# Three regroupings in a two-block transformer kernel: forget-gate panels first, memory-key sums between panels, and the inverse's transpose taken by turning

## The chip, the cores and the metric

The kernel runs on one core of one Trainium2 chip. The metric is the device time of one execution in microseconds, as the median of several runs. Five engines work side by side on the core, each through its own queue in order: TensorE (PE; its weight loads are PEld), VectorE (DVE), ScalarE (ACT), GpSimd (POOL) and SyncE (SP, which here only issues loads). They meet only at semaphores.

## The reference, cut to what matters

256 tokens of width 1024 run through two blocks in float32. The first block has four feed-forward layers, a mixer with a gated delta rule and retention, and a mixer with dilated and differential attention. The second has two layers, each with block-sparse attention, a gated recurrence (HGRN) and attention to 256 memory rows. The change touches three things.

The recurrence of the second block (`lb` is 0 in layer 0):

```
lb_all = jnp.cumsum(jax.nn.softmax(hgrn_lb_logits, axis=0), axis=0); lb_all = lb_all - lb_all[0:1]
qf = jax.nn.silu(q)
log_f = jnp.logaddexp(jnp.log(lb), jnp.log1p(-lb) + jax.nn.log_sigmoid(fl))
kf = (1.0 - lb) * jax.nn.sigmoid(-fl)
```

The keys of the memory: `km = rms_norm(k_m.reshape(B, M, MEM_HEADS, MEM_HEAD_DIM), mem_k_norm[l])`.

The delta rule, which for each tile of 128 tokens and each of four heads needs the inverse of a 128 by 128 unit triangular matrix. The kernel builds it from the 16 by 16 blocks on the diagonal, and then doubles the size of the block three times (steps s = 0, 1, 2).

## The kernel before, in words

All weights are cut on the host into panels of 128 by 2048 (1 MB). A panel passes four engines. SP loads it into one of three raw buffers. ACT rounds it to a high part (`split_hi`, L1557; in two halves `half_hi`, L1566). DVE forms the low part as the difference (`split_lo`, L1872; halves `half_lo`, L1855). PE multiplies it with the activations, which are split in the same way, in three products: L1047, L1048, L1049 for projections, 48 matmuls for a panel, 24 for a half. ACT then evacuates the result from PSUM (`evacuate`, L1657). A panel's split is queued three panels before its product.

The order of everything is written out once, in `order()`, as one list of steps (engine, kind, arguments); each engine walks through its own steps in that list, and waits for the step of another engine by its place in the list (`at`). `panel_list` gives the steps of a row of panels; `rounds` and `merge` lay chains of small steps side by side in rounds; `halves` cuts panels into two half products; `weave` puts these between the rounds, so that PE has a product while the small steps wait for each other.

**Second block, start of a layer.** Panels 0 and 1 of `in2_l` give the recurrence's q (with Silu on ACT), panels 2 and 3 its forget gate `fh`, 4 and 5 its values. After panel 3 ACT loads the table set of Exp and Ln (`logs`), and `last_mixer` begins:

- `f_abs` (DVE, L2217 and L2218): minus the absolute value of `fh`; in layer 1 also four operations on the logits of `lb`.
- `f_ln` (ACT, L1796 and L1797): Exp, then Ln of one plus that; in layer 1 the same on eight columns (L1799, L1800).
- `f_log` (DVE, L2231; L2239 is its last line): the logarithm of the sigmoid; in layer 1 also `lb` applied and the input of the second logarithm, seven operations; last the input of `k_gate`.
- layer 1 only: `f_ln2` (ACT, L1805 and L1806) and `f_log2` (DVE, L2244 and L2245).
- `k_gate` (ACT, L1810), `cum_f` (DVE, four scans L2250), `diagonal` (PE, L1304: two tiles of four heads, 16 matmuls), `diagonal_in` (DVE, L2256).
- then eight levels of `gap_f` (L2269, L2270), `decay_f` (ACT), `q_level` (DVE, L2279), `k_level` (POOL), `level` (PE, L1304), `level_in` (L2287), one for every two half panels.

The norm of the memory keys (units `sk0`, `sk1` of a layer) goes through the same first rounds: `cn_sq` (ACT square, L1747), `cn_sum` (PE with a matrix of ones, L1451), `cn_rstd` (ACT, L1755 and L1756), `cn_use` (DVE, L2125). In layer 1 PE's queue is: panels 0 to 3, half (4,0), `cn_sum` 0, half (4,1), `cn_sum` 1, halves (5,0), (5,1), (6,0), (6,1), `diagonal`, (7,0) ...

**First block, doubling of the inverse.** `m_mat` is the inverse so far, `t_mat` its transpose, both kept up to date. For each step and tile: `double_y` (PE: corner times `m_mat`), `y` (ACT copy from PSUM, L1710), `double` (PE: `t_mat` times y, and for s < 2 a second product that gives the transpose's correction), `doubled` (DVE, L2063: the subtraction on `m_mat`, and for s < 2 on `t_mat`). All products of four heads go through `heads` (L1304). A product of four heads is eight matmuls in the trace, a transpose of four heads is four. At the end of the stretch stand `evacuate` of `in0`'s panel 13 on ACT and `ret_out` on PE, which waits for it.

Of the kernel before, what the change touches and what calls it, by code (L numbers as in the profile page):

```python
# [345 lines left out]
def delta_rounds():  # L346
# [10 lines left out]
    for s in range(3):  # L357
        doubling += [both(("pe", "double_y", s), ("act", "y", s)),
                     both(("pe", "double", s), ("dve", "doubled", s), *([("pool", "corner", s + 1)] if s < 2 else []))]
# [8 lines left out]
def delta_tail():  # L368

    o = BASE["out0"]  # L370
    pe = [("double_y", 2, 0), ("double_y", 2, 1), ("double", 2, 0), ("double", 2, 1), ("ret_out", 0), ("ret_out", 1), ("u", 0),
          ("cn_sum", ("ro", 0)), ("state",), ("ret_out", 2), ("from_state",), ("ret_out", 3), ("u", 1), ("cn_sum", ("ro", 1)),
          ("delta_out", 0), ("delta_out", 1), ("out_part", "out0", 0, 0, 2), ("cn_sum", ("do", 0)), ("out_part", "out0", 0, 2, 4),
          ("cn_sum", ("do", 1)), ("out_part", "out0", 0, 4, 8), ("panel", "out0", 1), ("panel", "out0", 2), ("panel", "out0", 3)]
    act = [("y", 2, 0), ("y", 2, 1), ("evacuate", "in0", 13), ("half_hi", o + 1, 0), ("half_hi", o + 1, 1), ("cn_sq", ("ro", 0)), ("v_new", 0),
           ("cn_rstd", ("ro", 0)), ("state_copy",), ("half_hi", o + 2, 0), ("cn_sq", ("ro", 1)), ("v_new", 1), ("cn_rstd", ("ro", 1)),
           ("half_hi", o + 2, 1), ("cn_sq", ("do", 0)), ("cn_sq", ("do", 1)), ("cn_rstd", ("do", 0)), ("cn_rstd", ("do", 1)),
           ("split_hi", o + 3), ("split_hi", o + 4), ("split_hi", o + 5)]
    dve = [("doubled", 2, 0), ("doubled", 2, 1), ("half_lo", o + 1, 0), ("half_lo", o + 1, 1), ("v_less",), ("cn_use", ("ro", 0)),
           ("cn_use", ("ro", 1)), ("half_lo", o + 2, 0), ("half_lo", o + 2, 1), ("cn_use", ("do", 0)), ("cn_use", ("do", 1)),  # L380
           ("split_lo", o + 3), ("split_lo", o + 4)]
    return [(e, k, tuple(a)) for e, steps in (("pe", pe), ("act", act), ("dve", dve)) for k, *a in steps]


def hgrn_rounds(l):

    out = [[("dve", "f_abs", (l,)), ("act", "f_ln", (l,))], [("dve", "f_log", (l,))]]
    if l:
        out += [[], [("act", "f_ln2", (l,)), ("dve", "f_log2", (l,))]]
    out += [[("act", "k_gate", (l,)), ("dve", "cum_f", (l,))], [("pe", "diagonal", (l,)), ("dve", "diagonal_in", (l,))]]  # L390
# [31 lines left out]
def last_mixer(l):  # L422
# [6 lines left out]
    chains = [rounds(NORM_COLS, [(f"sk{l}", 0), (f"sk{l}", 1)]), hgrn,  # L429
# [54 lines left out]
def order():  # L484
# [49 lines left out]
    for l in range(2):  # L534
# [7 lines left out]
        angles = {1: [("dve", "angle", ())], 3: [("act", "sines", ())]} if l == 0 else None  # L542
        out += panel_steps(f"in2_{l}", angles, 0, 4) + [("act", "logs", ())] + last_mixer(l)
# [29 lines left out]
def build(nc, x_in, mem_in, pos_in, panels, gains, small_in, tab0, tab1, tab2, tab3, out):  # L573
    with ExitStack() as ctx:
# [248 lines left out]
        for k in range(2):  # L823
# [6 lines left out]
            for l in range(2):  # L830
                dest[f"in2_{l}", k] = (blocks(qh, k), "cols", ACT.Silu)
                dest[f"in2_{l}", 2 + k] = (blocks(fh, k), "cols", ACT.Copy)
# [132 lines left out]
        def _(sp):  # L965
# [9 lines left out]
            def load_panel(n):  # L975
# [10 lines left out]
                else:  # L986
                    source = {"gate": b + 3 * i - 1 if i else b, "up": b + 3 * i if i else b + 1, "both": b + 3 * UPS - 1, None: n}[kind]
                    if b == BASE["out0"]:
                        source = b + (n - b + 2) % 4
# [54 lines left out]
        def _(pe):  # L1044
# [330 lines left out]

            def double(s, t):
                pe.wait_ge(act_done, at("act", "y", s, t))
                ins = heads(ps[:, delta_bank(t, 1)], lambda h: t_mat[:, t, h], lambda h: pw_a[:, t, h])
                if s < 2:
                    ins = heads(ps[:, delta_bank(t, 0)], lambda h: pw_a[:, t, h], lambda h: t_mat[:, t, h])  # L1380
                ins.then_inc(pe_done, 1)
# [140 lines left out]
            def hgrn_out(l, g):  # L1522
                pe.wait_ge(dve_done, at("dve", "level_in", l, 7))
                for i in range(2):
# [10 lines left out]
                         "turn_m": turn_m, "kq": kq, "double_y": double_y, "double": double, "u": u, "state": state_mm,  # L1535
# [6 lines left out]
        def _(act):  # L1542
# [188 lines left out]

            def v_new_(t):
                act.wait_ge(pe_done, at("pe", "u", t))
                copy_back(v_new[:, t], t)
# [58 lines left out]
            def f_ln(l):  # L1793
# [4 lines left out]
                if l:  # L1798
# [13 lines left out]
            def decay_f(l, v):  # L1812
# [6 lines left out]
                          "decay": decay, "pow2_n": pow2_n, "pow4_n": pow4_n, "pow8_a": pow8_a, "t_rows": t_rows, "y": y,  # L1819
# [6 lines left out]
        def _(dve):  # L1826
# [259 lines left out]
            def doubled(s, t):  # L2086

                dve.wait_ge(pe_done, at("pe", "double", s, t))
                if s < 2:
                    add_to(t_mat[:, t], delta_bank(t, 0), ALU.subtract)  # L2090
# [123 lines left out]
            def f_abs(l):  # L2214

                dve.wait_ge(act_done, at("act", "evacuate", f"in2_{l}", 3))
                step(ts(hg[1], fh, -1.0, None, ALU.mult))  # L2217
                step(tt(hg[1], fh, hg[1], ALU.min))  # L2218
                if l:
# [8 lines left out]
            def f_log(l):  # L2228
# [3 lines left out]
                if l:  # L2232

                    step(stt(lbl, lbd, 0.0, lbn, ALU.min, ALU.subtract))
                    step(tt(hg[1], hg[1], along(lbl[:, 4:8], SEQ), ALU.add))
                    step(tt(hg[2], hg[1], along(lbl[:, 0:4], SEQ), ALU.subtract))
                    step(ts(hg[3], hg[2], -1.0, None, ALU.mult))
                    step(tt(hg[2], hg[2], hg[3], ALU.min))
# [42 lines left out]
            def level_in(l, v):  # L2281
# [6 lines left out]
                else:  # L2288
# [12 lines left out]
                          "angle": angle, "f_abs": f_abs, "f_log": f_log, "f_log2": f_log2, "cum_f": cum_f,  # L2301
# [73 lines left out]
```

## Time and profile before

| what | before |
|---|---|
| median of 3 runs (lowest, highest) | 1566.8 us (1565.97, 1567.17) |
| the profiled execution's own time | 1568.67 us |
| its span in the trace | 1566.7 us |
| PE, DVE, ACT, POOL busy, share of the span | 96%, 75%, 49%, 6% |
| granted clock of PE, mean | 0.997 of 2.4 GHz |

The span is the time from the first to the last instruction of one execution. A row of a timeline gives the start, the duration, the engine, the line of the kernel, and in square brackets how long the engine stood idle before it and which engine's result ended that. Matmuls overlap: the queue moves on before one has ended. Consecutive instructions of one line are merged, with their count behind x.

### The profile page before, as it was taken

How to read it: one execution, taken by the hardware profiler on the slowest of the kernel's cores; microseconds unless marked ns; L12 is line 12 of the kernel's file. 1: busy time of each engine (PE TensorE's matmuls, PEld its weight loads, DVE VectorE, ACT ScalarE, POOL GpSimd, SP SyncE). 2: the span in 40 equal slices, each digit the busy share in tenths (PEclk: the TensorE clock that was granted, in tenths of full speed). 3: DMA queues.
4: the chain of work that ended last, by engine and by line, in shares of the span. 5: the costliest groups of instructions: out<-in, count | busy, mean ns of one | idle time of the engine just before them, and what ended most of it. 6: DMA issues, size and time to landing. Idle time of an engine off the chain costs nothing.

```text
span 1566.7 us, 23942 instructions
## 1 busy us (share of the span) xinstructions
PE 1504.3 (96%) x9974; PEld 1347.7 (86%) x9974; DVE 1177.0 (75%) x1393; ACT 762.6 (49%) x931; POOL 94.1 (6%) x66
## 2 busy tenths in 40 slices
PE   7999999999999999999998999999999989989988
PEld 6888899988888888888886888889999869879967
DVE  6878668757887788787676788777779676579674
ACT  5433456435433453334545533345664675555662
POOL 2000000011000000000000100002013001003000
PEclk9999999999999999999999999999999999999999
DMA  7655534214655545555441465554444325434202
GB/s 263 213 188 188 180 132 174 81 55 157 212 189 200 177 173 188 191 189 185 170 153 55 162 212 189 189 188 162 155 169 137 106 82 187 162 110 161 108 28 81
DMA packets 51888, 246.76 MB, mean 157 GB/s; under 512 B 4619, under 2 KB 5771, under 8 KB 27718
## 3 DMA queue, kind: packets, MB, share of 16 engines
q1 hardware_dynamic: 50662, 238.29, 43.8%
q0 software_dynamic: 1120, 6.96, 1.2%
q8 instruction: 79, 1.29, 0.3%
q14 instruction: 27, 0.22, 0.0%
HBM read 244.18 MB, written 1.05 MB: 157 GB/s over the span
## 4 chain that ended last, share of the span: by engine, by line
PE 75%; DVE 13%; ACT 7%; issue 2%; DVEq 0%; ACTq 0%; POOL 0%
PE ps L1096 19%; PE ps L1098 9%; PE ps L1047 9%; PE ps L1049 9%; PE ps L1048 9%; PE ps L1149 8%; PE ps L1304 4%; PE ps L1150 4%; DVE w_lo L1872 3%; ACT w_hi L1557 2%; DVE act_two L1980 1%; ACT work L1766 1%; PE ps L1451 1%; ACT act_two L1635 1%; PE ps L1440 1%
## 5 line engine op out<-in xcount | busy, mean ns | idle before, releaser
L1557 ACT ACTIVATE w_hi<-raw 128x2048 fp32r<-128x2048 f32 x186 | 355.2, 1913 | 394.4 <-PE ps L1098 274.5
L1872 DVE TENSOR_TENSOR w_lo<-raw,w_hi 128x2048 fp32r<-128x2048 f32 x186 | 432.7, 2331 | 138.6 <-ACT w_hi L1557 135.9
L1096 PE MATMUL ps<-act_two,w_hi 128*128 128x512 f32 x1408 | 444.4, 397 | 5.0 <-DVE w_lo L1872 2.4
L1047 PE MATMUL ps<-act_two,w_hi 128*128 128x256 f32 x1120 | 327.8, 293 | 9.9 <-DVE act_two L1980 5.3
L1098 PEld LDWEIGHTS ps<-act_two,w_lo 128*128 128x128 f32 x1408 | 265.2, 188 | 63.0
L1048 PE MATMUL ps<-act_two,w_hi 128*128 128x256 f32 x1120 | 316.7, 283 | 0.0
L1049 PE MATMUL ps<-act_two,w_lo 128*128 128x256 f32 x1120 | 316.7, 283 | 0.0
L1098 PE MATMUL ps<-act_two,w_lo 128*128 128x256 f32 x1408 | 277.2, 278 | 0.0
L1047 PEld LDWEIGHTS ps<-act_two,w_hi 128*128 128x128 f32 x1120 | 214.6, 192 | 16.2 <-issue 5.4
L1096 PEld LDWEIGHTS ps<-act_two,w_hi 128*128 128x128 f32 x1408 | 215.1, 189 | 7.9 <-DVE w_lo L1872 3.6
L1048 PEld LDWEIGHTS ps<-act_two,w_hi 128*128 128x128 f32 x1120 | 214.7, 192 | 3.7 <-issue 3.6
L1049 PEld LDWEIGHTS ps<-act_two,w_lo 128*128 128x128 f32 x1120 | 214.5, 192 | 0.0
L1149 PE MATMUL ps<-g_two,w_hi 128*128 128x512 f32 x384 | 136.2, 398 | 0.0
L1855 DVE TENSOR_TENSOR w_lo<-raw,w_hi 128x1024 fp32r<-128x1024 f32 x76 | 103.9, 1393 | 26.2 <-ACT w_hi L1566 24.9
L1149 PE MATMUL ps<-act_two,w_hi 128*128 128x512 f32 x320 | 113.3, 398 | 3.1 <-DVE act_two L1911 2.5
L1150 PE MATMUL ps<-g_two,w_lo 128*128 128x256 f32 x384 | 107.5, 280 | 0.0
L1047 PE MATMUL ps<-w_hi,act_two 128*128 128x256 f32 (+1 forms) x336 | 106.1, 316 | 0.2 <-ACT work L1654 0.2
L1048 PE MATMUL ps<-w_lo,act_two 128*128 128x256 f32 (+1 forms) x336 | 100.1, 298 | 0.0
L1049 PE MATMUL ps<-w_hi,act_two 128*128 128x256 f32 (+1 forms) x336 | 100.1, 298 | 0.0
L1031 POOL TENSOR_TENSOR pair<-pair 128x512 f32<-128x512 f32 x27 | 41.0, 1520 | 860.3 <-ACT pair L1614 859.5
L1150 PE MATMUL ps<-act_two,w_lo 128*128 128x256 f32 x320 | 89.5, 280 | 0.0
L1149 PEld LDWEIGHTS ps<-g_two,w_hi 128*128 128x128 f32 x384 | 72.1, 188 | 16.9
(287 smaller groups left out, 2007.0 us busy)
## 6 DMA issues: line engine op xcount, KB each, us to landing
raw<-panels SPq DMA_DIRECT2D x184, 1024.0 KB, 4.8
raw<-panels SPq DMA_DIRECT2D x80, 512.0 KB, 4.8
raw<-panels SPq DMA_DIRECT2D x8, 256.0 KB, 6.3
table<-tab POOLq DMA_DIRECT2D x1, 1472.0 KB, 9.5
table<-tab POOLq DMA_DIRECT2D x1, 1216.0 KB, 5.5
xn<-x_in SPq DMA_DIRECT2D x4, 256.0 KB, 5.8
work<-mem_in POOLq DMA_DIRECT2D x1, 1024.0 KB, 9.0
xn<-mem_in POOLq DMA_DIRECT2D x1, 1024.0 KB, 5.2
```

Of the source, the lines that this page charges most:

```text
L1031: nc.gpsimd.tensor_tensor(pair[:, 0:512], pair[:, 0:512], pair[:, 512 * b:512 * b + 512], ALU.add).then_inc(pool_done, 1)
L1047: pe.matmul(o, l[0], r[0], start=start, stop=False, skip_group_check=shared)
L1048: pe.matmul(o, l[0], r[1], start=False, stop=False, skip_group_check=shared)
L1049: return pe.matmul(o, l[1], r[0], start=False, stop=stop, skip_group_check=shared)
L1096: pe.matmul(grid(ps[:, bank + half], 2), w[half][0], act_two[:, slots[c]], start=c == 0, stop=False)
L1098: ins = pe.matmul(ps[:, bank + half, 0:SEQ], w[half][1], act_hi[:, slots[c]], start=False, stop=c == DC - 1)
L1149: pe.matmul(grid(ps[:, bank], 2), hi, two, start=first and m == 0, stop=False)
L1150: ins = pe.matmul(ps[:, bank, 0:SEQ], lo, two[:, 0], start=False, stop=last and m == len(quarters) - 1)
L1304: ins = pe.transpose(oh, lhs(h), ident) if turn else pe.matmul(oh, lhs(h), rhs(h), start=True, stop=True)
L1557: nc.scalar.activation(w_hi[:, s], raw[:, s], ACT.Copy).then_inc(panel_hi, 1)
L1855: ins = tt(w_lo[:, s, c], raw[:, s, c], w_hi[:, s, c].bitcast(F32), ALU.subtract)
L1872: tt(w_lo[:, s], raw[:, s], w_hi[:, s].bitcast(F32), ALU.subtract).then_inc(panel_lo, 1)
```

## The change

- The weights of the forget gate become panels 0 and 1 of `in2_l`, those of q (Silu) panels 2 and 3. SP loads the first four panels in rotated order; the host's layout stays.
- `f_abs` runs on DVE beside panel 2, after that panel's queued `split_lo`, as one operation on `fh` instead of two.
- The small operations for `lb` (four on DVE in `f_abs`, two on ACT in `f_ln`, the last on DVE in `f_log`) are done in layer 0 and kept for layer 1.
- In layer 1 `f_log` has three operations: it leads straight to the second logarithm. Two others, `lb` added and the input of `k_gate`, become the step `f_gate`, which DVE does after it. `f_ln2` stands on ACT behind the evacuation of panel 4 and its splits, as before.
- The squares of the memory keys stand on ACT after the splits beside panels 0 and 1, their sums on PE behind panels 1 and 2. `cn_rstd` of the two units follows in `f_log`'s round (in layer 1 the second follows `f_ln2`), and both `cn_use` come after `cum_f` on DVE.
- In the delta rule `double` has one product in all steps. For s = 1 and 2, `turn_again` on PE turns `m_mat` into PSUM behind `double_y`, and `t_again` on ACT copies it to `t_mat` behind `y`; `double` waits for it.

The diff, without the lines that only register the new steps:

```diff
@@ -355,7 +355,7 @@
     for s in range(3):
-        doubling += [both(("pe", "double_y", s), ("act", "y", s)),
+        doubling += [both(("pe", "double_y", s), *([("pe", "turn_again", s)] if s else []), ("act", "y", s), *([("act", "t_again", s)] if s else [])),
                      both(("pe", "double", s), ("dve", "doubled", s), *([("pool", "corner", s + 1)] if s < 2 else []))]
@@ -368,11 +368,11 @@
     o = BASE["out0"]
-    pe = [("double_y", 2, 0), ("double_y", 2, 1), ("double", 2, 0), ("double", 2, 1), ("ret_out", 0), ("ret_out", 1), ("u", 0),
+    pe = [("double_y", 2, 0), ("turn_again", 2, 0), ("double_y", 2, 1), ("turn_again", 2, 1), ("double", 2, 0), ("double", 2, 1), ("ret_out", 0), ("ret_out", 1), ("u", 0),
           ("cn_sum", ("ro", 0)), ("state",), ("ret_out", 2), ("from_state",), ("ret_out", 3), ("u", 1), ("cn_sum", ("ro", 1)),
           ("delta_out", 0), ("delta_out", 1), ("out_part", "out0", 0, 0, 2), ("cn_sum", ("do", 0)), ("out_part", "out0", 0, 2, 4),
           ("cn_sum", ("do", 1)), ("out_part", "out0", 0, 4, 8), ("panel", "out0", 1), ("panel", "out0", 2), ("panel", "out0", 3)]
-    act = [("y", 2, 0), ("y", 2, 1), ("evacuate", "in0", 13), ("half_hi", o + 1, 0), ("half_hi", o + 1, 1), ("cn_sq", ("ro", 0)), ("v_new", 0),
+    act = [("y", 2, 0), ("t_again", 2, 0), ("y", 2, 1), ("t_again", 2, 1), ("evacuate", "in0", 13), ("half_hi", o + 1, 0), ("half_hi", o + 1, 1), ("cn_sq", ("ro", 0)), ("v_new", 0),
            ("cn_rstd", ("ro", 0)), ("state_copy",), ("half_hi", o + 2, 0), ("cn_sq", ("ro", 1)), ("v_new", 1), ("cn_rstd", ("ro", 1)),
@@ -384,10 +384,13 @@
 
-    out = [[("dve", "f_abs", (l,)), ("act", "f_ln", (l,))], [("dve", "f_log", (l,))]]
+    key_norm = [[("act", "cn_rstd", ((f"sk{l}", g),)), ("dve", "cn_use", ((f"sk{l}", g),))] for g in (0, 1)]
+    out = [[("act", "f_ln", (l,))], [("dve", "f_log", (l,)), key_norm[0][0]]]
     if l:
-        out += [[], [("act", "f_ln2", (l,)), ("dve", "f_log2", (l,))]]
-    out += [[("act", "k_gate", (l,)), ("dve", "cum_f", (l,))], [("pe", "diagonal", (l,)), ("dve", "diagonal_in", (l,))]]
+        out += [[("dve", "f_gate", (l,))], [("act", "f_ln2", (l,)), ("dve", "f_log2", (l,)), key_norm[1][0]]]
+    else:
+        out[1] += key_norm[1][:1]
+    out += [[("act", "k_gate", (l,)), ("dve", "cum_f", (l,)), key_norm[0][1], key_norm[1][1]], [("pe", "diagonal", (l,)), ("dve", "diagonal_in", (l,))]]
     ahead = len(out)
@@ -426,7 +429,7 @@
     h = n + 7
-    chains = [rounds(NORM_COLS, [(f"sk{l}", 0), (f"sk{l}", 1)]), hgrn,
+    chains = [hgrn,
               [[]] * n + rounds(NORM_COLS, qk + [(f"ho{l}", 0), (f"ho{l}", 1)]),
@@ -539,8 +542,12 @@
         out += [product] + scaled(f"pre{l}") + [evacuate] + late
-        angles = {1: [("dve", "angle", ())], 3: [("act", "sines", ())]} if l == 0 else None
-        out += panel_steps(f"in2_{l}", angles, 0, 4) + [("act", "logs", ())] + last_mixer(l)
+        square, total = [[(e, k, ((f"sk{l}", g),)) for g in (0, 1)] for e, k in (("act", "cn_sq"), ("pe", "cn_sum"))]
+        beside = {0: square[:1], 1: total[:1] + square[1:], 2: total[1:] + [("dve", "f_abs", (l,))], 3: []}
+        if l == 0:
+            beside[1] = beside[1] + [("dve", "angle", ())]
+            beside[3] = [("act", "sines", ())]
+        out += panel_steps(f"in2_{l}", beside, 0, 4) + [("act", "logs", ())] + last_mixer(l)
         if l == 0:
@@ -828,8 +835,8 @@
             for l in range(2):
-                dest[f"in2_{l}", k] = (blocks(qh, k), "cols", ACT.Silu)
-                dest[f"in2_{l}", 2 + k] = (blocks(fh, k), "cols", ACT.Copy)
+                dest[f"in2_{l}", k] = (blocks(fh, k), "cols", ACT.Copy)
+                dest[f"in2_{l}", 2 + k] = (blocks(qh, k), "cols", ACT.Silu)
                 dest[f"in2_{l}", 4 + k] = (rows(ih, k), "rows", ACT.Copy)
@@ -986,6 +993,8 @@
                     if b == BASE["out0"]:
+                        source = b + (n - b + 2) % 4
+                    if b in (BASE["in2_0"], BASE["in2_1"]) and n - b < 4:
                         source = b + (n - b + 2) % 4
@@ -1373,12 +1382,13 @@
 
+            def turn_again(s, t):
+                pe.wait_ge(dve_done, at("dve", "doubled", s - 1, t))
+                heads(ps[:, delta_bank(t, 1)], lambda h: m_mat[:, t, h], None, turn=True).then_inc(pe_done, 1)
+
             def double(s, t):
-                pe.wait_ge(act_done, at("act", "y", s, t))
-                ins = heads(ps[:, delta_bank(t, 1)], lambda h: t_mat[:, t, h], lambda h: pw_a[:, t, h])
-                if s < 2:
-                    ins = heads(ps[:, delta_bank(t, 0)], lambda h: pw_a[:, t, h], lambda h: t_mat[:, t, h])
-                ins.then_inc(pe_done, 1)
+                pe.wait_ge(act_done, at("act", "t_again" if s else "y", s, t))
+                heads(ps[:, delta_bank(t, 1)], lambda h: t_mat[:, t, h], lambda h: pw_a[:, t, h]).then_inc(pe_done, 1)
 
@@ -1729,6 +1739,10 @@
 
+            def t_again(s, t):
+                act.wait_ge(pe_done, at("pe", "turn_again", s, t))
+                copy_back(t_mat[:, t], delta_bank(t, 1))
+
             def v_new_(t):
@@ -1795,7 +1809,7 @@
                 ins = nc.scalar.activation(hg[1], hg[1], ACT.Ln, bias=cst("one"))
-                if l:
+                if not l:
                     step(nc.scalar.activation(lbn, lbn, ACT.Exp))
@@ -2086,8 +2100,6 @@
                 dve.wait_ge(pe_done, at("pe", "double", s, t))
-                if s < 2:
-                    add_to(t_mat[:, t], delta_bank(t, 0), ALU.subtract)
                 finish(add_to(m_mat[:, t], delta_bank(t, 1), ALU.subtract))
@@ -2213,10 +2225,9 @@
 
-                dve.wait_ge(act_done, at("act", "evacuate", f"in2_{l}", 3))
-                step(ts(hg[1], fh, -1.0, None, ALU.mult))
-                step(tt(hg[1], fh, hg[1], ALU.min))
-                if l:
+                dve.wait_ge(act_done, at("act", "evacuate", f"in2_{l}", 1))
+                step(stt(hg[1], fh, -1.0, fh, ALU.mult, ALU.min))
+                if not l:
                     a, b = sm("lb", 0, 4), sm("lb", 4, 4)
@@ -2230,12 +2241,16 @@
                 if l:
-
+                    step(tt(hg[2], hg[1], along(lbd[:, 0:4], SEQ), ALU.add))
+                    finish(stt(hg[2], hg[2], -1.0, hg[2], ALU.mult, ALU.min))
+                else:
+                    tt(k_g, hg[1], fh, ALU.subtract)
                     step(stt(lbl, lbd, 0.0, lbn, ALU.min, ALU.subtract))
-                    step(tt(hg[1], hg[1], along(lbl[:, 4:8], SEQ), ALU.add))
-                    step(tt(hg[2], hg[1], along(lbl[:, 0:4], SEQ), ALU.subtract))
-                    step(ts(hg[3], hg[2], -1.0, None, ALU.mult))
-                    step(tt(hg[2], hg[2], hg[3], ALU.min))
+                    finish(tt(lbd[:, 0:4], lbl[:, 4:8], lbl[:, 0:4], ALU.subtract))
+
+            def f_gate(l):
+
+                step(tt(hg[1], hg[1], along(lbl[:, 4:8], SEQ), ALU.add))
                 finish(tt(k_g, hg[1], fh, ALU.subtract))
```

## Rows read from the trace of the kernel before

**Rows 1.** The page: busy times, and the chain that ended last by engine.
```profile
PE 1504.3 (96%) x9974; PEld 1347.7 (86%) x9974; DVE 1177.0 (75%) x1393; ACT 762.6 (49%) x931; POOL 94.1 (6%) x66
...
PE 75%; DVE 13%; ACT 7%; issue 2%; DVEq 0%; ACTq 0%; POOL 0%
```

**Rows 2.** Windows: length, PE, PEld, DVE, ACT, POOL busy, clock, DMA.
```profile
1112.00:1150.00 38.00, 38.00 (x309) 37.04 (x309) 27.57 (x36) 26.42 (x29) 0.00 (x0) 1.00 0.44 152
...
1366.00:1398.00 32.00, 24.82 (x181) 23.26 (x180) 23.35 (x28) 20.34 (x25) 0.00 (x0) 0.95 0.29 99
...
1396.00:1397.00 1.00, 1.00 (x7) 1.00 (x6) 1.00 (x2) 1.00 (x2) 0.00 (x0) 0.50 0.00 0
```

**Rows 3.** Timeline of PE: delta rule, then both layers.
```profile
312.41 1.53 PE L1304 MATMUL ps<-const,work 128*128 128x128 f32 x12 [0.23 <-DVE work L2063]
...
337.38 1.95 PE L1304 MATMUL ps<-work 128*128 128x128 f32 x16
...
1149.39 1.95 PE L1304 MATMUL ps<-work 128*128 128x128 f32 x16
...
1372.35 1.12 PE L1451 MATMUL ps<-pair,const 128*128 128x512 f32 x2 [1.55 <-ACT pair L1747]
...
1378.61 1.13 PE L1451 MATMUL ps<-pair,const 128*128 128x512 f32 x2 [2.27 <-ACT pair L1747]
...
1394.60 3.65 PE L1304 MATMUL ps<-work 128*128 128x128 f32 x16 [3.35 <-ACT work L1810]
...
1398.00 0.37 PE L1047 MATMUL ps<-act_two,w_hi 128*128 128x256 f32 x1
...
1415.35 1.95 PE L1304 MATMUL ps<-work,xn 128*128 128x128 f32 x16
...
1422.90 1.95 PE L1304 MATMUL ps<-work,xn 128*128 128x128 f32 x16
```

**Rows 4.** Timeline of ACT: delta rule, then layer 1.
```profile
338.47 0.60 ACT L1710 ACTIVATE work<-ps 128x512 f32<-128x512 f32 x1 [8.85 <-PE ps L1304]
...
1356.44 0.60 ACT L1657 ACTIVATE work<-ps 128x512 f32<-128x512 f32 x1 [1.74 <-PE ps L1049]
...
1368.45 1.90 ACT L1557 ACTIVATE w_hi<-raw 128x2048 fp32r<-128x2048 f32 x1
...
1370.37 1.28 ACT L1685 ACT_TABLE_LOAD   x1
...
1371.67 0.63 ACT L1747 ACTIVATE pair<-work 128x512 f32<-128x512 f32 x1
...
1375.37 1.06 ACT L1796 ACTIVATE work<-work 128x1024 f32<-128x1024 f32 x1 [3.07 <-DVE stat L2226]
...
1376.46 1.15 ACT L1797 ACTIVATE work<-work,const 128x1024 f32<-128x1024 f32 x1
```

**Rows 5.** Timeline of DVE: layer 0, then layer 1.
```profile
1143.53 1.22 DVE L2239 TENSOR_TENSOR work<-work 128x1024 f32<-128x1024 f32 x1
...
1370.39 2.29 DVE L1872 TENSOR_TENSOR w_lo<-raw,w_hi 128x2048 fp32r<-128x2048 f32 x1 [3.47 <-ACT w_hi L1557]
...
1379.90 0.75 DVE L2125 SCALAR_TENSOR_TENSOR work<-work,small,pair 128x512 f32<-128x512 f32 x1 [4.56 <-ACT pair L1756]
...
1388.70 2.36 DVE L1855 TENSOR_TENSOR w_lo<-raw,w_hi 128x1024 fp32r<-128x1024 f32 x2
...
1394.63 2.43 DVE L2250 TENSOR_TENSOR_SCAN work<-table,work 128x256 f32<-128x256 f32 x4
...
1398.28 1.29 DVE L2256 TENSOR_TENSOR work<-ps,const 128x512 f32<-128x512 f32 x2
...
1410.28 1.23 DVE L2279 TENSOR_TENSOR work<-work,pair 128x1024 f32<-128x1024 f32 x1
...
1417.31 1.22 DVE L2279 TENSOR_TENSOR work<-work,pair 128x1024 f32<-128x1024 f32 x1
```

**Rows 6.** Chain of waits, delta rule: start, duration, what.
```profile
319.90 3.57 PE ps L1304 x32
```

More of the change, by code:

```diff
@@ L1534, in _ @@
                          "turn_k": turn_k, "kk": kk, "turn_a": turn_a, "pow2": pow2, "pow4": pow4, "pow8": pow8, "pow16": pow16,
-                         "turn_m": turn_m, "kq": kq, "double_y": double_y, "double": double, "u": u, "state": state_mm,
+                         "turn_m": turn_m, "kq": kq, "double_y": double_y, "double": double, "turn_again": turn_again, "u": u, "state": state_mm,
                          "from_state": from_state, "delta_out": delta_out, "ret_scores": ret_scores, "ret_out": ret_out,
@@ L1818, in _ @@
                           "evacuate": evacuate, "silu": silu, "logs": logs_and_exps, "tap": tap, "conv_silu": conv_silu, "ab_exp": ab_exp, "softplus": softplus,
-                          "decay": decay, "pow2_n": pow2_n, "pow4_n": pow4_n, "pow8_a": pow8_a, "t_rows": t_rows, "y": y,
+                          "decay": decay, "pow2_n": pow2_n, "pow4_n": pow4_n, "pow8_a": pow8_a, "t_rows": t_rows, "t_again": t_again, "y": y,
                           "v_new": v_new_, "state_copy": state_copy, "cn_sq": cn_sq, "cn_rstd": cn_rstd, "exp": exp_,
@@ L2300, in _ @@
                           "gate_out": gate_out, "y_lo": y_lo, "mask_max": mask_max, "divide": divide, "lam_mul": lam_mul, "lam": lam,
-                          "angle": angle, "f_abs": f_abs, "f_log": f_log, "f_log2": f_log2, "cum_f": cum_f,
+                          "angle": angle, "f_abs": f_abs, "f_log": f_log, "f_log2": f_log2, "f_gate": f_gate, "cum_f": cum_f,
                           "diagonal_in": diagonal_in, "gap_f": gap_f, "q_level": q_level, "level_in": level_in})
```

## The prediction, made before the changed kernel ran

> **What bounds the kernel now.** I read the page's busy times first. The reader is to see a kernel that lives on TensorE: PE is busy 1504.3 us of 1566.7, and the chain that ended last is 75% PE, 13% DVE, 7% ACT [rows 1]. So shorter DVE or ACT work is worth only what PE waits for it, and each edit has to be read in its own stretch. There are three: the delta rule of the first block (about 296 to 346 us), and the first panels of the two layers of the second block (about 1112 to 1150 and 1348 to 1400).
>
> By windows, the first layer shows PE busy 38.00 us of 38: nothing can be won there except by less PE work. The second layer's twin stretch has 24.82 of 32 [rows 2]. The timeline of PE says where that goes: 1.55 us before the first sum of memory keys, 2.27 before the second, 3.35 before `diagonal`; and `diagonal` takes 3.65 us where the same 16 matmuls of `level` take 1.95 [rows 3]. The clock is the reason: the window inside it has the granted clock at 0.50 (1.2 GHz), after a pause of 3.35 us [rows 2, 3].
>
> Why layer 1 only? It has a second logarithm. The chain of waits there runs evacuate of panel 3, `split_hi`, `split_lo`, `f_abs`, `f_ln`, `f_log`, `f_log2`, `k_gate`, `diagonal`. ACT's square for the first sum is queued behind a table load, the one for the second behind `f_ln` [rows 4]; `f_abs` is queued behind a `split_lo` that ends at 1370.39 + 2.29 = 1372.68, and `f_ln` starts at 1375.37: 2.7 us for `f_abs` alone [rows 4, 5].
>
> **The change, layer 1.** PE's order becomes panel 0, 1, sum, 2, sum, 3, then half panels (4,0) to (6,1), `diagonal`. The sums are moved, not removed: at 1.0 us each (1.12 here with a restart) [rows 3] they put off panel 3's end from 1367.9 (the first sum's start 1372.35, less 1.55, less a half of 2.9) to 1369.9. Six halves follow without a sum between them. A half costs 2.9: the second sum starts at 1378.61, four halves then end at 1394.60 - 3.35 = 1391.25, so (1391.25 - 1379.6)/4 [rows 3]. PE is ready for `diagonal` at 1369.9 + 17.3 = 1387.2.
>
> The chain to `k_gate`, each term by its row. `split_hi` starts 1368.45 + 2.0 = 1370.45, takes 1.9; table load 1.28; Exp 1.06 and Ln 1.15 (the small pair is in layer 0 now): `f_ln` ends 1375.9 [rows 4]. `f_abs` is long done beside panel 2 and leaves the chain. `f_log` is three operations on 1024 columns at 1.24 with their gap (1.23 is the row of one): 1379.65. The new `f_gate` adds 2 x 1.24: 1382.15. The two `split_lo` halves of the next panel, queued on DVE between `f_gate` and `f_log2`, take 2.36: 1384.5. `f_ln2` is done by 1382 on ACT beside them. `f_log2` 2 x 1.24: 1387.0 [rows 5]. `k_gate` 1.06: 1388.1. So PE waits 0.9 to 1.0 us instead of 3.35, and after so short a pause I take the clock to stay at 1.00: the other pauses of 1.5 to 2.3 us here were not followed by a `diagonal`-like slowdown (the sum after 2.27 us took 1.13) [rows 3]. `diagonal` then holds the queue 1.8 us, and half (7,0) starts at 1389.9, not at 1398.00. **Gain 8.1 us.** Bounds: 9.1 if the wait vanishes; 4.9 if DVE is what the rest follows (next paragraph).
>
> Is the gain kept? DVE is behind PE afterwards. After `f_log2` come a `split_lo` half (1.18), `cum_f` 2.43, the two `cn_use` of the keys that now stand here (0.75 each; they left an earlier place with idle time around it), another half: `diagonal_in` starts at 1393.4 instead of 1398.28, only 4.9 earlier. `q_level` of level 0 would end 1411.5 - 4.9 = 1406.6, and PE wants level 0 at 1415.35 - 8.1 = 1407.25 [rows 3, 5]. That is a margin of 0.65 us, thin; but DVE's levels come 7.03 apart and PE's 7.55 (1410.28 to 1417.31, 1415.35 to 1422.90) [rows 3, 5], so it grows by 0.5 per level. I keep the whole 8.1.
>
> The squares now have to be ready when PE reaches the sums. After panel 0 ACT idles 1.74 us before it can evacuate panel 1 [rows 4], a square is 0.6, and the first Silu's table load (1.28) has moved from before panel 0's evacuation to panel 2's: 2.4 us of slack. The late Silu evacuation holds up nothing PE reads before panel 4. SP loads the same four panels in rotated order; no bytes change, POOL's queue gets nothing new.
>
> **Layer 0.** Same moves; the operations on eight columns come here from layer 1, and the pass of `f_abs` that only negated goes. `angle` stays on DVE beside panel 1. `f_log` ended at 1143.53 + 1.22 = 1144.75 and `diagonal` ran at 1149.39 [rows 3, 5], 4.6 us apart, with `k_gate` and one pair of halves between; `f_log` loses the wait for `f_abs` and gains under 1 us of small operations, and PE has no idle to return. **0 us** (bounds -0.5 to +0.5, the small operations' size).
>
> **The delta rule.** `double` ran two products of four heads for steps 0 and 1; four calls in 3.57 us, 0.89 each [rows 6]. The second product goes in both steps and both tiles: 4 x 0.89 = 3.57 off PE. Added: four `turn_again`, transposes of four heads; 12 such transposes (three calls) took 1.53 us, so about 0.45 each with the tail shared: 1.8 [rows 3]. Net **1.8 us**, in a stretch without PE idle, so all of it shows. The four `add_to` off DVE are hidden. Four `t_again` copies of 0.60 are added to ACT, and `double` waits for them: a first `y` starts 1.1 us after its product starts (337.38, 338.47) [rows 3, 4], so y, t, y, t end at about 1.7, 2.2, 3.0 and 3.5 us, and PE reaches the second `double` at 2 x (0.89 + 0.45) + 0.89 = 3.57. It fits by nothing; a tenth or two may be lost. Behind `t_again` on ACT stands the evacuation of in0's panel 13, for which `ret_out` waits: it ends some 4.4 after the start, `ret_out` comes at 4.5. Bounds of this part: 0 (a transpose at a product's price) to 2.5.
>
> On that price, TensorE: Matmul & The Clock Gate (the Trainium skill), Part 4, says a transpose took about 275 ns in a kernel's context and that the fast clock does not engage for transposes. Sixteen at 275 ns would be 4.4 us and the delta part a loss of 0.8. The rows have 12 in 1.53 us in a busy queue, so I go by them.
>
> On the table load, ScalarE: Activation LUTs (the Trainium skill), What ACT_TABLE_LOAD costs, adds a drain of about 1.38 us to the load's 1.28. The load after panel 3 stands on this chain, and by the page `diagonal` would wait 2.4, not 1.0. In the trace the square follows the load within 0.02 us (1371.67 after 1370.37 + 1.28) [rows 4], so the sum has 1.28.
>
> **Sum.** 1.8 + 8.1 + 0 = 9.9 us. Profiled execution: span 1566.7, run 1568.67, median of the runs 1566.8, so the run's excess lies outside the span and the median stands 1.9 below it. Span after 1556.8; median 1566.8 - 9.9 = **1556.9 us**.
>
> **Rivals.**
> - *DVE takes the gain.* The 0.65 us margin at level 0 is wrong, PE stalls there and layer 1 gives 4.9 (DVE's shift). For: DVE's queue in the levels is nearly full. Against: its period is 0.5 shorter. 1566.8 - 4.9 - 1.8 = 1560.1. Chance 0.13.
> - *The copies take the delta gain.* `double` waits for `t_again` in both steps; 1566.8 - 8.1 = 1558.7. For: the tie above. Chance 0.09.
> - *The change does not do what it says:* `diagonal` still waits 3.3 us, since `split_hi` of panel 3 and the new `f_gate` keep the chain. Then 2.3 of wait and the 1.8 of slow clock stay: 9.9 - 4.1 = 5.8, so 1561.0. Chance 0.05.
> - *Transposes lower the clock.* If PE at a transpose counted as resting, the delta's products would run at 1.2 GHz for a spell like that of `diagonal`: 1.7 us back, 1558.6. Against: these products ran at full pace (0.89) within 10 us of twelve transposes [rows 3, 6]. Chance 0.03. The page of the clock gate named above has such a rule, in Part 4.
> - *Slower: the sums block PE.* Each of four sums now stands in PE's queue between panels and waits for a square behind a `split_hi`, which waits for a panel to land. Beyond the slack of 2.4 us each microsecond is paid four times; from 2.4 + 9.9/4 = 4.9 us late the gain is gone, at 6 us late the time is 1571. The split for panel 3 shows no wait for a landing in the trace. Chance 0.02.
> - The forecast itself: 0.68, with its own range 1555.5 to 1558.5.
>
> Within 0.2% (3.1 us, about what a measurement of this kernel can tell from no change) only a mixture of the bad cases would end: 0.03. Faster 0.95, slower 0.02. The range goes from 1554.0 (9.1 and 2.5, rounded, with half a microsecond from layer 0) to 1560.7 (DVE takes the gain, and the delta gains less).
>
> **What will show it.** In layer 1 PE has no wait before the two sums, which stand between panels; one of 0.5 to 1.5 us before `diagonal`, which takes 1.95; the granted clock never leaves 1.00 there; level 0 follows its halves without a pause. In layer 0 PE stays full. In the delta stretch `doubled` is one operation on DVE and two `y` alternate with two `t_again` on ACT, and everything behind it stands 1.8 us earlier. It would be wrong if PE waits for ACT at a sum, if `level` waits for `q_level`, or if `k_gate` stands later than 1388 less the delta's gain.

## The result, and the profile after

The changed kernel takes **1556.98 us** (median of 4 runs, 1556.16 to 1557.66) against 1566.38 for the one before in the same series; the ratio is 0.9939, 95% interval 0.9927 to 0.9950. Forecast: 1556.9. The profiled execution has a span of 1555.8 us, 10.9 less. Of these, 0.7 us lie ahead of every edit (the waits for the first inputs were shorter), so the edits account for 10.2 in the trace; the medians differ by 9.4, and the forecast gain of 9.9 lies between. That the medians hit the forecast time within 0.1 us is partly luck (the section on the experiments shows how much executions vary).

The page of the changed kernel, busy times and the chain that ended last, beside [rows 1]:

```profile
PE 1500.2 (96%) x9958; PEld 1344.4 (86%) x9958; DVE 1171.9 (75%) x1387; ACT 763.8 (49%) x935; POOL 93.9 (6%) x66
...
PE 75%; DVE 12%; ACT 7%; issue 2%; DVEq 0%; ACTq 0%; POOL 0%
```

PE's busy time fell by 4.1 us, in part work that is gone and in part the slow spell of `diagonal`; the other 6.8 are waits that are gone. Windows of layer 0's first panels, of layer 1's, and of the three microseconds around `diagonal`:

```profile
1110.00:1148.00 38.00, 38.00 (x309) 37.04 (x309) 28.66 (x41) 26.49 (x32) 0.00 (x0) 1.00 0.47 167
1363.00:1387.00 24.00, 23.06 (x193) 22.86 (x192) 19.38 (x17) 17.20 (x20) 0.00 (x0) 1.00 0.39 132
1384.00:1387.00 3.00, 2.06 (x18) 1.86 (x17) 2.96 (x5) 2.87 (x4) 0.00 (x0) 1.00 0.63 262
```

Layer 0 is as full as in [rows 2]. In layer 1 PE idles 0.94 us in 24 where it idled 7.2 in 32, and the clock stays at 1.00. The timeline of PE of the changed kernel, from the delta rule to level 1 (the row at 1346.36 is PE's last wait for the residual norm, ahead of panel 0 of layer 1; it is my zero for layer 1; before the change it stands at 1348.94). In the first rows x8 is `double_y`, x4 `turn_again` and x16 the two `double`:

```profile
334.84 0.60 PE L1313 MATMUL ps<-const,work 128*128 128x128 f32 x4
335.27 1.06 PE L1313 MATMUL ps<-work 128*128 128x128 f32 x8
336.17 0.60 PE L1313 MATMUL ps<-const,work 128*128 128x128 f32 x4
336.60 2.06 PE L1313 MATMUL ps<-work,xn 128*128 128x128 f32 x16
...
343.71 1.16 PE L1313 MATMUL ps<-work 128*128 128x128 f32 x8 [0.34 <-ACT work L1720]
...
1146.90 1.95 PE L1313 MATMUL ps<-work 128*128 128x128 f32 x16
...
1346.36 0.39 PE L1056 MATMUL ps<-act_two,w_hi 128*128 128x256 f32 x1 [0.69 <-DVE act_two L1994]
...
1353.65 1.02 PE L1461 MATMUL ps<-pair,const 128*128 128x512 f32 x2
...
1360.26 1.02 PE L1461 MATMUL ps<-pair,const 128*128 128x512 f32 x2
...
1385.24 2.05 PE L1313 MATMUL ps<-work 128*128 128x128 f32 x16 [0.94 <-ACT work L1824]
...
1387.05 0.37 PE L1056 MATMUL ps<-act_two,w_hi 128*128 128x256 f32 x1
...
1404.40 1.95 PE L1313 MATMUL ps<-work,xn 128*128 128x128 f32 x16
```

The sums stand between the panels with no wait. Half (7,0) starts at 1387.05 instead of 1398.00 [rows 3], 10.95 earlier; 2.58 of that came from ahead of layer 1, so layer 1 gave 8.37. Level 0 is also 10.95 earlier, and from there to the end of the kernel it is 151.37 us against 151.39, so nothing was given back. The delta rule gave 1.78: from the twelve transposes (now 311.68) to the product behind panel 13 it is 32.03 us, before 33.81 (312.41 and 346.22). ACT and then DVE of the changed kernel, on the way to `k_gate` and to level 0:

```profile
1369.48 1.28 ACT L1695 ACT_TABLE_LOAD   x1
1370.77 1.06 ACT L1810 ACTIVATE work<-work 128x1024 f32<-128x1024 f32 x1
...
1376.83 1.06 ACT L1819 ACTIVATE work<-work 128x1024 f32<-128x1024 f32 x1 [0.19 <-DVE work L2245]
...
1384.13 1.06 ACT L1824 ACTIVATE work<-work 128x1024 f32<-128x1024 f32 x1 [2.39 <-DVE work L2260]
```

```profile
1373.05 1.23 DVE L2242 SCALAR_TENSOR_TENSOR work<-work 128x1024 f32<-128x1024 f32 x1 [1.19 <-ACT work L1811]
...
1379.34 2.36 DVE L1869 TENSOR_TENSOR w_lo<-raw,w_hi 128x1024 fp32r<-128x1024 f32 x2
...
1382.87 1.23 DVE L2260 TENSOR_TENSOR work<-work 128x1024 f32<-128x1024 f32 x1
...
1402.45 1.23 DVE L2294 TENSOR_TENSOR work<-work,pair 128x1024 f32<-128x1024 f32 x1
```

`f_log` starts at 1373.05, its three operations and `f_gate`'s two run without a pause, the halves of the next panel stand from 1379.34 to 1381.6 in front of `f_log2`, and `k_gate` waits for it. `q_level` ends at 1403.68, 0.72 us ahead of level 0.

### The profile page after: what moved, and what is told of

Read it like the earlier page. It is cut to its first block, busy times and chain, and to the rows that moved or that the text cites. A ratio compares the mean times of both kernels' runs of the same rounds, so it can differ in the third digit from the quotient of the medians.

```text
span 1555.8 us, 23909 instructions
## 1 busy us (share of the span) xinstructions
PE 1500.2 (96%) x9958; PEld 1344.4 (86%) x9958; DVE 1171.9 (75%) x1387; ACT 763.8 (49%) x935; POOL 93.9 (6%) x66
## 4 chain that ended last, share of the span: by engine, by line
PE 75%; DVE 12%; ACT 7%; issue 2%; DVEq 0%; ACTq 0%; POOL 0%
PE ps L1105 19%; PE ps L1107 10%; PE ps L1056 9%; PE ps L1058 9%; PE ps L1057 9%; PE ps L1158 8%; PE ps L1313 4%; PE ps L1159 4%; DVE w_lo L1886 3%; ACT w_hi L1567 2%; DVE act_two L1994 1%; ACT work L1780 1%; PE ps L1461 1%; ACT act_two L1645 1%; PE ps L1450 1%
## 5 line engine op out<-in xcount | busy, mean ns | idle before, releaser
L1869 DVE TENSOR_TENSOR w_lo<-raw,w_hi 128x1024 fp32r<-128x1024 f32 x76 | 103.5, 1388 | 27.4 <-ACT w_hi L1576 26.1
```

What stands on the lines that cost most here:

```text
L1869: ins = tt(w_lo[:, s, c], raw[:, s, c], w_hi[:, s, c].bitcast(F32), ALU.subtract)
```

## The experiments

How they are read: a stretch that no edit touches (from the product behind panel 13, 343.71 in the changed kernel, to the zero of layer 0, PE's last wait for the residual norm there, 1109.11) took between 763.1 and 766.7 us in the fourteen profiles. (It took 765.38 us before and 765.40 after, so the spans of these two profiles may be compared.) Spans and medians therefore can't settle an edit of 1 or 2 us. Differences inside one stretch repeat to a few hundredths, so layer 1 is read from its zero to `diagonal` and to level 0.

Most of that variation is TensorE's clock. Between 828 and 865 us PE waits 1.49, 0.82, 1.03, 1.34, 1.22 and 1.48 us with little work between, in all fourteen profiles within 0.02 us, but the clock falls at different places. Windows of the kernel before, then of the changed one, each behind the wait of 1.34 and behind the one of 1.48:

```profile
855.50:858.50 3.00, 2.98 (x9) 2.28 (x10) 1.36 (x7) 1.22 (x3) 0.00 (x0) 0.50 0.00 0
864.60:867.60 3.00, 3.00 (x25) 3.00 (x26) 2.90 (x4) 1.11 (x1) 0.00 (x0) 1.00 0.01 3
```

```profile
853.10:856.10 3.00, 3.00 (x14) 1.94 (x15) 1.32 (x7) 1.95 (x5) 0.00 (x0) 1.00 0.00 0
861.00:864.00 3.00, 3.00 (x16) 3.00 (x16) 2.90 (x4) 0.74 (x1) 0.00 (x0) 0.50 0.00 0
```

The piece from the wait of 1.49 to the wait of 1.48 takes 32.1 to 32.3 us in the four profiles with a slow spell behind the wait of 1.34, and 30.8 in the ten others; the hundred matmuls behind it take 13.5 to 13.6 in the five with one at the wait of 1.48, and 12.1 in the nine others. A slow spell at about 832, as ten profiles have, costs nothing there: the four profiles without it have one more wait, of 0.86 us.

**One part alone: the delta rule.** The kernel before, with this and no more:

```
-  ins = heads(ps[:, delta_bank(t, 1)], t_mat, pw_a)
-  if s < 2: ins = heads(ps[:, delta_bank(t, 0)], pw_a, t_mat)
+  turn_again: heads(ps[:, delta_bank(t, 1)], m_mat, None, turn=True)
+  t_again:    copy_back(t_mat[:, t], delta_bank(t, 1))
```

> The kernel before with the edit of the delta rule alone. Theory: four products of 0.89 go and four transposes of 0.45 come, all of it in a stretch where PE has no idle: the time falls by 1.8 us, to about 1564.6, and everything behind 346 us stands 1.8 us earlier. Rival: the copies that the second product now waits for take it back (0 us), or part of it.

1565.52 us against 1566.19, ratio 0.9992 (0.9982 to 1.0001): too small for the runs, not for the trace. The same stretch takes 32.03 us, 1.78 less:

```profile
344.32 1.16 PE L1304 MATMUL ps<-work 128*128 128x128 f32 x8 [0.34 <-ACT work L1711]
...
1375.91 2.07 PE L1452 MATMUL ps<-pair,const 128*128 128x512 f32 x2 [2.27 <-ACT pair L1752]
...
1391.89 2.95 PE L1304 MATMUL ps<-work 128*128 128x128 f32 x16 [1.83 <-ACT work L1815]
```

The wait behind panel 13 is the same 0.34 as before; no copy holds up PE. The two other rows are a surprise: layer 1 is not touched here, yet the clock fell at the second sum. Windows of this kernel there:

```profile
1376.00:1378.00 2.00, 2.00 (x4) 0.97 (x5) 0.78 (x2) 1.05 (x2) 0.00 (x0) 0.50 0.00 0
...
1394.00:1396.00 2.00, 2.00 (x11) 2.00 (x11) 1.97 (x3) 1.16 (x2) 0.00 (x0) 0.50 0.00 0
```

After 2.27 us of wait the clock stood at 0.50 here, and at 1.00 in the profile of before (the sum took 1.13 there [rows 3]). The slow spell made PE reach `diagonal` later, so the wait there was 1.83, not 3.35; `diagonal` started 45.64 us from the zero (1346.25 here), as before (45.66). The chain through DVE and ACT sets that start, PE's clock does not.

**One part alone: the second block.** The changed kernel with the old delta rule.

> The changed kernel with the old delta rule: all edits of the second block, no others. Theory: 8.1 to 8.4 us faster than before (1558.2 or so), all of it from the first panels of layer 1; with the delta edit alone it adds up to the whole change. Rival: the edits depend on each other, and the two gains do not add up to 9.4 to 9.9.

1557.32 us, ratio 0.9943 (0.9929 to 0.9956). Zero to level 0: 58.06 us, against 58.04 in the changed kernel and 66.41 before. The parts add up in the trace: 8.35 and 1.78 are 10.13, and the edits together gave 10.15.

**Chain without sums, sums without chain.** Old delta rule in both.

```
 chain_only:  chains = [rounds(NORM_COLS, [(f"sk{l}", 0), (f"sk{l}", 1)]), hgrn, ...
              beside = {2: [("dve", "f_abs", (l,))]}
 sums_only:   beside = {0: square[:1], 1: total[:1] + square[1:], 2: total[1:]}
              f_abs, f_ln, f_log, f_log2 and the order of panels as before
```

> The edits of the second block without the moved sums: squares and sums of the memory keys stay where they were, beside panel 4; forget gate panels first, f_abs beside panel 2, the short chain with f_gate. Old delta rule. Theory: the chain sets the end. Square 0 comes before f_ln (0.6 on the chain), the first sum still waits 1.5 us, the second no longer, since f_ln does not wait for f_abs; diagonal does not wait. So 7.5 us faster than before, 0.6 to 0.9 less than with the moved sums. Rival: the two waits at the sums (3.8 us) are a gain of their own, and this kernel is only 4.3 to 4.6 us faster.

> The kernel before with the squares and sums of memory keys beside panels 0 to 2 and nothing else (query panels first, f_abs behind panel 3, the old long f_log). Theory: PE loses its two waits at the sums (3.8 us) and pays them all back at diagonal, since the chain through panel 3 is what ends last; two sums of 1.0 us now stand ahead of panel 3 and put the chain off by 2.0 less the square (0.6) that left it: 1.4 us slower than before, with diagonal waiting about 8 us. Rival: the waits at the sums are won by themselves: 3.8 us faster.

Chain alone: 1561.72 us, ratio 0.9967 (0.9954 to 0.9979); `diagonal` at 41.05 us from zero (before 45.66, both 38.89), level 0 at 60.22, that is 6.19 of the 8.35. Expected were 7.5 and no wait at `diagonal`; it waits 1.28. Sums alone: 1567.35 us, 1.0006 (0.9998 to 1.0015); `diagonal` at 44.03, level 0 at 65.18. Expected was a loss of 1.4, it is a gain of 1.2 in the stretch. Most of that is lost again in layer 0, where PE of this kernel waits for an evacuation and `diagonal` starts 38.56 us from the layer's zero (37.79 in the thirteen other profiles):

```profile
1143.03 0.39 PE L1054 MATMUL ps<-act_two,w_hi 128*128 128x256 f32 x1 [0.52 <-ACT work L1664]
```

From the zero of layer 0 to level 0 of layer 1 it is 303.43 us against 303.75 before, and the runs show no gain. Both misses in layer 1 have one main cause, which DVE of the chain-only kernel shows:

```profile
1376.83 0.75 DVE L2131 SCALAR_TENSOR_TENSOR work<-work,small,pair 128x512 f32<-128x512 f32 x1 [3.47 <-ACT pair L1762]
1377.62 1.23 DVE L2236 SCALAR_TENSOR_TENSOR work<-work 128x1024 f32<-128x1024 f32 x1
```

The first row is `cn_use` of the memory keys, the second `f_log`. `f_log`'s logarithm is done at 1375.04, but `cn_use` stands ahead of it in DVE's queue and waits for the sum and `cn_rstd`: 2.6 us. A second `cn_use` (0.79) stands inside the chain. In the kernel before it is the same: `f_ln` ends at 1378.0, the `cn_use` stands at 1379.90 [rows 5], and `f_log` starts behind it at 1380.68. So the moved sums are worth something because `cn_use` moves behind `f_log2`, not because PE stops waiting for them. (This is read from the queues; a kernel that moves `cn_use` alone was not run.) With the sums alone PE's 3.8 us of waits do come back at `diagonal`, as expected:

```profile
1392.61 3.78 PE L1311 MATMUL ps<-work 128*128 128x128 f32 x16 [5.45 <-ACT work L1817]
```

The evacuation of panel 3, in the kernel before and with the sums alone, shows what the sums ahead of it cost:

```profile
1367.96 0.60 ACT L1657 ACTIVATE work<-ps 128x512 f32<-128x512 f32 x1 [3.36 <-PE ps L1049]
```

```profile
1369.29 0.60 ACT L1664 ACTIVATE work<-ps 128x512 f32<-128x512 f32 x1 [4.21 <-PE ps L1056]
```

From their zeros (1348.94 and 1348.58) that is 19.02 and 20.71: 1.69 for two sums, less than the expected 2.0, since the queue moves on before a sum has ended. The square that left counts for nothing, because ACT idled 3.07 us between it and the Exp [rows 4]. So the start of `diagonal` moved by +1.69, -2.53 and -0.79 (the two `cn_use`): -1.63, as measured.

**How long a wait, and what clock.** One and two redundant operations in layer 1, and the second kernel again:

```
 def f_log2(l):
+    for _ in range(N): step(tt(hg[3], hg[1], hg[2], ALU.add))
```

> The changed kernel with one redundant DVE operation (1.25 us) at the head of f_log2 of layer 1, so that k_gate comes 1.25 later and diagonal waits about 2.2 us instead of 0.94. DVE and PE shift together, so the margin at level 0 stays. Theory of the prediction: a pause of 2.2 us does not lower the clock; diagonal keeps 1.95 us, and 1.25 us is all it costs. Rival, from the run of the delta edit alone, where the clock stood at 0.50 after a wait of 2.27 us: the clock falls, diagonal takes 2.9 to 3.7, and it costs 2.2 to 3.0.

> The same with two redundant operations (2.5 us): diagonal waits about 3.45 us, as it did before the change (3.35). Theory: the clock falls to 0.50 again and diagonal takes about 3.65, so it costs 2.5 of wait and 1.7 of slow clock, 4.2 us; half of what layer 1 gained is gone. Rival: what lowered the clock before was not the last wait but all the waits since panel 3 (7.2 us in 22), of which one is left: diagonal stays at 1.95, and the cost is 2.5.

> The kernel with two redundant operations in f_log2 once more, for a second profiled execution of it. Its first profile showed 3.46 us of wait at diagonal and the clock at 1.00 all the same; its ten timed executions lie between 1558.6 and 1563.0, five of them within 1.9 us of the fastest or so and the others above. Theory: whether the clock falls after such a wait differs from execution to execution; this profile shows diagonal at 1.95 to 2.05 or at 3.0 to 3.7, and the span goes with it. Rival: the clock never falls here after one wait, and the spread has another place.

N = 1: 1557.9 us, ratio 0.9955 (0.9940 to 0.9969); N = 2: 1561.41, 0.9974 (0.9964 to 0.9984). `diagonal` in the kernels with N = 1, N = 2 and N = 2 again:

```profile
1385.20 2.05 PE L1313 MATMUL ps<-work 128*128 128x128 f32 x16 [2.21 <-ACT work L1824]
```

```profile
1386.08 2.05 PE L1313 MATMUL ps<-work 128*128 128x128 f32 x16 [3.46 <-ACT work L1824]
```

```profile
1387.92 3.04 PE L1313 MATMUL ps<-work 128*128 128x128 f32 x16 [3.47 <-ACT work L1824]
```

With N = 1 level 0 stands 59.32 us from zero, 1.28 more than in the changed kernel: the added operation and nothing else. With N = 2 it is the same program, the same wait, and two clocks; the window 1386 to 1388 of the first N = 2 profile has 1.00, the window 1388 to 1392 of the second 0.60:

```profile
1388.00:1392.00 4.00, 4.00 (x22) 4.00 (x23) 3.90 (x8) 3.18 (x4) 0.00 (x0) 0.60 0.02 4
```

Level 0 stands there 60.57 and 62.15 us from zero: 2.53 and 4.11 more than in the changed kernel. The slow spell costs 1.6 us, in some executions. So neither expectation for N = 2 holds as it stands: the first profile shows no fall of the clock, and the second shows one although only this wait is left. The ten timed executions of N = 2 (1558.58 to 1562.95) fit both, but their spread alone does not prove it, since untouched stretches spread as much.

**The order of `f_gate` and the halves.**

```
 gate_inside:  f_log(1) = min/subtract, hg[2] add, hg[1] add, k_g subtract, hg[2] min
 log2_first:   ORDER: f_log2 directly behind f_gate, ahead of half_lo (7,0), (7,1)
```

> The changed kernel with the two operations of f_gate back inside f_log of layer 1, ahead of the second logarithm. Theory: f_ln2 starts 2.5 us later, at 1379.4 by the trace of the changed kernel, and ends at 1381.6, when DVE has just done the two split_lo halves (1381.6) that stand ahead of f_log2 anyway: within 0.2 us of the changed kernel. The moved pair is hidden by the halves. Rival: the second logarithm comes onto the chain and costs its own length, 2.2 us.

> The changed kernel with f_log2 of layer 1 ahead of the two split_lo halves in DVE's queue (2.3 us of another panel's work). Theory: k_gate starts 2.3 us earlier, PE does not wait at diagonal any more, and the layer gains the 0.94 us that are left: span 0.9 shorter. Rival: the halves are needed by the panel behind diagonal, PE waits for them instead, and nothing is gained.

`f_gate` inside: 1556.63 us, 0.9947 (0.9932 to 0.9962); `diagonal` 38.89 us from zero, after 0.95 of wait: no difference. DVE does the same operations up to the halves, and the logarithm fits beside them. `f_log2` first: 1555.1 us, 0.9936 (0.9921 to 0.9951); `diagonal` starts 37.78 from zero without a wait, 1.1 earlier. But level 0 is at 57.37, only 0.67 earlier, since DVE is now late:

```profile
1401.68 2.05 PE L1316 MATMUL ps<-work,xn 128*128 128x128 f32 x16 [0.36 <-DVE work L2297]
```

**DVE's margin, and the price of a transpose.** Two redundant operations behind the scans of layer 1; and each `turn_again` twice.

> The changed kernel with two redundant DVE operations (2.5 us) behind the scans of layer 1, that is behind everything that diagonal waits for. Theory: PE has 0.72 us of margin at level 0, so it waits 1.8 us there, and no more at the later levels, since DVE's levels come 0.5 closer than PE's. Rival: the halves in DVE's queue are what PE needs first; it waits at a panel before level 0, or again at later levels, and the whole 2.5 us come through.

> The changed kernel with each of the four turn_again done twice. Theory: a transpose of four heads costs 0.45 us in a full queue, so the stretch of the delta rule grows by 1.8 us (from 32.03 to 33.8 between the twelve transposes and the first product behind panel 13). Rival: the product after it hides or stretches the transposes (the queue waits for the copies anyway), and it grows by less than 1.2 or by more than 2.5.

With DVE 2.5 us later (one timed run, 1557.3 us), level 0 comes 1.69 later (59.73 from zero), and it stays at that. PE of this kernel:

```profile
1397.00 0.39 PE L1056 MATMUL ps<-act_two,w_hi 128*128 128x256 f32 x1 [0.30 <-ACT work L1667]
...
1403.74 2.05 PE L1313 MATMUL ps<-work,xn 128*128 128x128 f32 x16 [0.73 <-DVE work L2296]
```

The size is as expected, the place only in part. The pause at 1397.00 costs 0.56 us, one at the half at 1390.71 (0.01 idle) 0.25, and the one at level 0 0.88: a restart of PE costs more than the idle time in brackets, which begins only when the last matmul has ended. So 0.8 of the 1.69 arise at half panels ahead of level 0, as the rival had it. With the transposes doubled (one timed run, 1556.32 us), the delta stretch takes 33.73 us (310.96 to 344.69), 1.70 more: 0.43 for four.

**A version with more of the chain ahead.**

```
 beside[1]:  f_abs (ahead of split_lo), f_ln, f_log      beside[2]:  f_gate
 rounds:     f_ln2 where f_ln was, then f_log2
```

> The changed kernel with more of the chain of layer 1 moved ahead: f_abs as soon as panel 1 is evacuated, f_ln in ACT's idle time before it evacuates panel 2 (2.39 us, and the log table is still loaded), f_log and f_gate beside panels 1 and 2, f_ln2 where f_ln was. Theory: the wait at diagonal (0.94) goes, as with f_log2 ahead of the halves, and the 0.36 us that PE then waited for q_level at level 0 do not come back, since DVE's work is earlier and not only in another order: from the second wait for the residual norm to level 0 57.1 us instead of 58.04. Rival: the evacuation of panel 2 comes late behind f_ln and its table load, a panel waits for its split, and the gain is less than with f_log2 first (0.67).

1556.84 us against 1567.01, ratio 0.9936 (0.9922 to 0.9950). ACT of this kernel, between the square and panel 2's evacuation:

```profile
1355.99 1.05 ACT L1814 ACTIVATE work<-work 128x1024 f32<-128x1024 f32 x1
1357.08 1.15 ACT L1815 ACTIVATE work<-work,const 128x1024 f32<-128x1024 f32 x1
1358.25 1.28 ACT L1671 ACT_TABLE_LOAD   x1
1359.79 0.60 ACT L1671 ACTIVATE work<-ps 128x512 f32<-128x512 f32 x1 [0.25 <-PE ps L1062]
```

The logarithm fits into that idle time; `diagonal` starts 37.79 us from zero without a wait, level 0 at 56.85, 1.19 earlier than in the changed kernel and 0.5 earlier than with `f_log2` first. In this stretch it is the shortest of all, and both figures are those of layer 0 (37.79 and 56.85 from its zero), where PE is full: nothing is left to win there by moving waits. 1.2 us are less than these timed runs can tell from the changed kernel.

## Why the prediction was right, and where it was not

- **Layer 1, 8.1 forecast, 8.37 measured.** `k_gate` ends at 1385.19; forecast 1388.1 less the 2.5 that came from ahead. The 0.4 between them are mostly the sums, priced at 2.0 us for two and measured at 1.68 (panel 3 is evacuated 20.70 us from the zero). PE waits 0.94 (0.9 to 1.0). The clock stays, `diagonal` takes its full pace, half (7,0) comes at 1387.05 (1387.4 by the same shift).
- **The list of the chain was incomplete.** It went from `f_ln` to `f_log` and left out the `cn_use` between them and the one behind `f_log`. Its sum for after was right, because both had left the chain; the cause given for the old length (`f_abs` alone, 2.7 us) was less than half of it. Link by link, `diagonal` starts 6.77 us earlier from the zero: -3.7 for `f_abs` (from the end of the table load to the Exp), -3.3 for the two `cn_use`, -1.5 for the operations for `lb` and the shorter `f_log`, +1.7 for the sums; the slow spell that is gone makes it 8.37. Mainly for this reason the chain-only and sums-only kernels missed by 1.3 and 2.6 us.
- **The clock step rested on a row that does not hold.** "After so short a pause I take the clock to stay" came from a wait of 2.27 us with no slow spell behind it [rows 3]. The same wait in the kernel with the delta edit alone had one. What did hold is the wait of 0.94 to 0.95, in all five profiles in which it occurred.
- **Kept gain: right.** Margin 0.72 (forecast 0.65). The rival that DVE takes the gain was near: with 2.5 us more on DVE 1.7 come through to level 0, and with `f_log2` first 0.36 of wait appear.
- **Delta rule: 1.8 forecast, 1.78 measured**, alone and together. The copies fit: `double` follows the transposes in the full queue. Doubling gives 0.106 us for one transpose, so the 275 ns of TensorE: Matmul & The Clock Gate (the Trainium skill), Part 4, are not what it costs here. They agree with its duration: the profile has 0.27 us for a single transpose, and the next one starts 0.11 us after it; in a full queue the distance counts. That the fast clock does not engage for transposes, as the same part says, this trace contradicts. Transposes of the attention in the kernel before, at a granted clock of 0.50 and at 1.00, start 0.21 and 0.11 us apart:

```profile
855.79 0.42 PE L1477 MATMUL ps<-const,work 128*128 128x128 f32 x1
856.00 0.42 PE L1482 MATMUL ps<-const,work 128*128 128x128 f32 x1
...
859.91 0.27 PE L1477 MATMUL ps<-const,work 128*128 128x128 f32 x1
860.02 0.27 PE L1482 MATMUL ps<-const,work 128*128 128x128 f32 x1
```

- **Layer 0: 0 forecast.** From the zero of layer 0 (1111.60 before, 1109.11 after) to `diagonal` 37.79 in both.
- **Squares: slack 2.4 forecast.** The first square ends at 1351.20 and its sum stands at 1353.65: 2.45. That sums block PE when squares are later than this was not tried.
- **Table load.** The load starts 0.02 us after the split ahead of it (1367.56 + 1.90), and the Exp at 1370.77 follows the load (1369.48 + 1.28) by 0.01 us; the drain of 1.38 that ScalarE: Activation LUTs (the Trainium skill), What ACT_TABLE_LOAD costs, adds to it does not show, and `diagonal` waited 0.94, not 2.4.
- **The range.** Its lower end is said to be 9.1, 2.5 and 0.5 us; these give 1554.7, not 1554.0.

## What to carry to other kernels

To price a chain, write down everything in the queue of each engine between two of its links, also what belongs to another calculation: here `cn_use` of the memory keys held `f_log` for 2.6 us, and no edit of the chain itself would have found it. A wait of TensorE that is followed by a longer wait on the same chain is worth nothing by itself (3.8 us of waits at the sums came back at `diagonal`). And when untouched stretches vary by 3 us, here mostly because the clock falls in one execution and not in another, test an edit of 1 us between two landmarks around it.

## What the runs showed of the hardware

The granted clock after a pause of PE is not a function of the pause. In the first panels of layer 1, waits of 0.94, 1.28, 1.55 and 2.21 us kept 1.00; 2.27 kept it in one profile and lost it in another; 1.83 lost it, in the one profile where it had been lost at the second sum too; 3.46 and 3.47 in one and the same program kept and lost it; 3.35 and 5.45 lost it. With the clock at 0.50 (1.2 GHz) for all or part of it, `diagonal` took 2.95 to 3.78 us instead of 1.95 to 2.05. So a wait of 2 to 3.5 us before 16 small matmuls costs up to 1.6 us on top, in some executions; what decides between them stays open.

Nor is 2 us a safe bound. Between 828 and 865 us, where waits of 0.8 to 1.5 us follow each other closely, every profile has at least one slow spell: at the wait of 1.34 us the clock fell in four of fourteen profiles, and at the wait of 1.48 in five.

Transposes follow the granted clock like other matmuls: 0.42 us each and 0.21 apart at 0.50, 0.27 and 0.11 at 1.00.
